# Fourteen interleaved units of each MLP without a loop; copies and sums of odd up groups moved ahead of the seventh product's splits

## What is computed

```python
def squared_relu_mlp(x, w1, w2):
    return jnp.square(jax.nn.relu(x @ w1)) @ w2
...
        h = layer_norm(DN_ALPHA * h + y, ln_g[i, 0], ln_b[i, 0])
        f = squared_relu_mlp(h, mlp_w1[i], mlp_w2[i])
        h = layer_norm(DN_ALPHA * h + f, ln_g[i, 1], ln_b[i, 1])
```

## Time and profile before

| what | us |
|---|---|
| median of 3 runs | 2150.74 |
| lowest and highest | 2150.31 and 2152.03 |
| profiled execution, its own time | 2150.6 |
| its span in the profile | 2148.9 |

### The profile page before, as it was taken

The page is one execution under the profiler, slowest core; times in us unless marked ns, Lnnn a source line. Parts: engine busy times, 40 slices in busy tenths (PEclk is TensorE's granted clock), DMA queues, the critical chain, the costliest instruction groups (busy, mean ns, idle before and its releaser), DMA issues.

```text
span 2148.9 us, 28041 instructions
## 1 busy us (share of the span) xinstructions
PE 2123.4 (99%) x10994; PEld 1817.2 (85%) x10994; DVE 1721.2 (80%) x1456; ACT 1163.7 (54%) x1034; POOL 185.5 (9%) x153
## 2 busy tenths in 40 slices
PE   9999999999999999999999999999999999999998
PEld 8888888988888888888888888889888888888886
DVE  5555559888988988989777666797988988989887
ACT  4444445456656655656554344445655656566562
POOL 3000000300000000000030111102000000000000
PEclk9999999999999999999999999999999999999999
DMA  9546547678988889888646544666789889888883
GB/s 304 176 140 204 171 151 242 198 233 239 258 245 267 241 229 285 233 246 223 247 158 217 180 156 157 236 213 215 209 242 269 255 230 259 251 246 250 228 267 137
DMA packets 237310, 478.51 MB, mean 223 GB/s; under 512 B 7616, under 2 KB 7616, under 8 KB 236176
## 3 DMA queue, kind: packets, MB, share of 16 engines
q1 hardware_dynamic: 204672, 406.09, 53.9%
q0 software_dynamic: 32096, 70.07, 17.8%
q10 hardware_dynamic: 432, 0.79, 0.1%
HBM read 474.81 MB, written 2.10 MB: 222 GB/s over the span
## 4 chain that ended last, share of the span: by engine, by line
PE 95%; DVE 2%; ACT 1%; issue 1%; DMA 0%; ACTq 0%; POOL 0%; DVEq 0%
PE ps L609 66%; PE ps L935 8%; PE ps L933 8%; PE ps L939 7%; PE ps L813 2%; PE ps L868 1%; PE ps L870 1%; PE ps L875 1%; ACT hi L1361 1%; DVE work L1982 1%; PE ps L680 1%; DVE lo L1950 0%; ACT work L1372 0%; DMA res<-in_x_dram 0%; DVE res L1740 0%
## 5 line engine op out<-in xcount | busy, mean ns | idle before, releaser
L609 PE MATMUL ps<-X,hi 128*128 128x512 f32 (+1 forms) x3008 | 699.8, 378 | 15.3 <-DVE work L1982 9.6
L609 PEld LDWEIGHTS ps<-X,hi 128*128 128x128 f32 x3008 | 549.0, 189 | 119.9 <-issue 14.4
L1361 ACT ACTIVATE hi<-raw 128x2048 fp32r<-128x2048 f32 x196 | 372.6, 1915 | 238.7 <-DVE raw L1964 146.3
L1950 DVE TENSOR_TENSOR lo<-raw,hi 128x2048 fp32r<-128x2048 f32 x196 | 443.6, 2286 | 14.5 <-PE ps L609 6.5
L1569 DVE TENSOR_TENSOR lo<-raw,hi 128x2048 fp32r<-128x2048 f32 x136 | 314.0, 2323 | 127.1 <-ACT hi L1159 125.6
L1159 ACT ACTIVATE hi<-raw 128x2048 fp32r<-128x2048 f32 x151 | 287.3, 1915 | 209.7 <-PE ps L609 163.2
L609 PE MATMUL ps<-X,lo 128*128 128x256 f32 x2816 | 387.1, 283 | 0.2 <-issue 0.2
L609 PEld LDWEIGHTS ps<-X,lo 128*128 128x128 f32 x2816 | 373.2, 191 | 13.1 <-issue 0.3
L1950 DVE TENSOR_TENSOR lo<-up_raw,hi 128x2048 fp32r<-128x2048 f32 x112 | 256.1, 2287 | 56.6 <-PE ps L609 32.6
L1345 ACT ACTIVATE hi<-up_raw 128x2048 fp32r<-128x2048 f32 x112 | 214.0, 1911 | 94.5 <-PE ps L939 83.7
L609 PE MATMUL ps<-hi,X 128*128 128x512 f32 x768 | 245.0, 394 | 0.0
(11 more groups left out here) (237 smaller groups left out, 2345.6 us busy)
## 6 DMA issues: line engine op xcount, KB each, us to landing
raw<-in_mlp_w_dram SPq DMA_DIRECT2D x144, 1024.0 KB, 7.6
up_raw<-in_mlp_w_dram SPq DMA_DIRECT2D x112, 1024.0 KB, 7.6
raw<-in_mlp_w_dram POOLq DMA_DIRECT2D x56, 1024.0 KB, 9.4
raw<-in_gla_w_in_dram SPq DMA_DIRECT2D x48, 1024.0 KB, 5.3
raw<-in_attn_w_qkv_dram SPq DMA_DIRECT2D x47, 1024.0 KB, 5.2
raw<-in_attn_w_o_dram SPq DMA_DIRECT2D x16, 1024.0 KB, 5.9
raw<-in_gla_w_o_dram SPq DMA_DIRECT2D x16, 1024.0 KB, 5.3
work<-in_ln_g_dram POOLq DMA_DIRECT2D x4, 1024.0 KB, 6.7
```

Source lines behind the costliest of these rows:

```text
L609: return pe.matmul(o, w, m, start=start, stop=stop)
L1361: act.activation(hi[:, P_AT[p] % 4], raw[:, slot], ACT.Copy).then_inc(hi_ready, 2 if p == PRODUCTS - 1 else 1)
L1950: dve.tensor_tensor(lo[:, at % 3], src, hi[:, at % 4].bitcast(F32), ALU.subtract).then_inc(lo_ready, n)
```

## The change

The loop over units 4 to 11 is gone on the three engines, and all fourteen units are written out. On ScalarE the copies of an odd unit (`right_halves(n, 1, 0, ...)`) stand ahead of `down_hi(m, i, c, 6)`. On VectorE the sums of an odd unit (`add_halves(n, 1, 0)`) and then `add_product(m, i, c, 4)` stand ahead of `down_lo(m, i, c, 6)`. Line numbers in the new kernel are lower by 5 to 11.

```diff
--- before.py
+++ after.py
@@ -1027,13 +1027,8 @@
                             w = mm(ps[:, 4 + i, 0:SEQ], lo[:, (j + 2) % 3, k, blk(i)], X[:, 4 * j + k, 0, :],
                                    False, 4 * j + k == KT - 1)
                     w.then_inc(w_used, 1)
-                for c in range(4):
-                    fused(m, c, c, c == 0)
-                with pe.Fori(1, FGS // 4) as it:
-                    for c in range(4):
-                        fused(m, 4 * it + c, c)
-                for c in range(FGS % 4):
-                    fused(m, FGS - FGS % 4 + c, c)
+                for i in range(FGS):
+                    fused(m, i, i % 4, i == 0)
                 g, r = g0 + 2 + FG * FGS, r0 + PRODUCTS * FGS
                 pe.wait_ge(res_added, r - 2)
                 rest_tiles(g, ((6, 7), (5, 4)), ((0, 0), (0, 1), (1, 0), (1, 1)),
@@ -1427,16 +1422,15 @@
                 up_hi(m, i, 3)
                 down_hi(m, i, c, 4)
                 down_hi(m, i, c, 5)
+                right_halves(n, 1, 0, used, k - 2, formed + 4)
                 down_hi(m, i, c, 6)
                 if end:
                     f = i + 1 + (G_MLP[m] + 2 - AHEAD_MLP[m])
                     split_hi(g + FG, 0, f)
-                    right_halves(n, 1, 0, used, k - 2, formed + 4)
                     split_hi(g + FG, 1, f)
                     squared_relu(n, 1, k, half)
                     return
                 up_hi(m, i + 1, 0)
-                right_halves(n, 1, 0, used, k - 2, formed + 4)
                 down_hi(m, i + 1, nxt, 0)
                 squared_relu(n, 1, k, half)
                 up_hi(m, i + 1, 1)
@@ -1453,13 +1447,8 @@
                 up_hi(m, 0, 1)
                 right_halves(n0 + 1, 1, 1, 4 * g0 + 8, None, None)
                 squared_relu(n0 + 1, 1, 32 * m + 2, 0)
-                for c in range(4):
-                    fused(m, c, c)
-                with act.Fori(1, FGS // 4) as it:
-                    for c in range(4):
-                        fused(m, 4 * it + c, c)
-                for c in range(FGS % 4):
-                    fused(m, FGS - FGS % 4 + c, c, True)
+                for i in range(FGS):
+                    fused(m, i, i % 4, i >= FGS - 2)
                 g, f = g0 + 2 + FG * FGS, f0 + 2 + FGS
                 split_hi(g, 2, f)
                 split_hi(g, 3, f)
@@ -2082,14 +2071,13 @@
                 add_product(m, i, c, 2)
                 down_lo(m, i, c, 4)
                 down_lo(m, i, c, 5)
+                add_halves(n, 1, 0)
+                add_product(m, i, c, 4)
                 down_lo(m, i, c, 6)
-                add_product(m, i, c, 4)
                 if last:
                     tail_lo(m, 0)
-                    add_halves(n, 1, 0)
                     return
                 up_lo(m, i + 1, 0)
-                add_halves(n, 1, 0)
                 down_lo(m, i + 1, nxt, 0)
 
             def tail_lo(m, j):
@@ -2116,17 +2104,9 @@
                 up_lo(m, 0, 0)
                 down_lo(m, 0, 0, 0)
                 add_halves(n0 + 1, 1, 1)
-                even_unit(m, 0, 0, True)
-                odd_unit(m, 1, 1)
-                even_unit(m, 2, 2)
-                odd_unit(m, 3, 3)
-                with dve.Fori(1, FGS // 4) as it:
-                    even_unit(m, 4 * it, 0)
-                    odd_unit(m, 4 * it + 1, 1)
-                    even_unit(m, 4 * it + 2, 2)
-                    odd_unit(m, 4 * it + 3, 3)
-                even_unit(m, FGS - 2, 0)
-                odd_unit(m, FGS - 1, 1, True)
+                for i in range(0, FGS, 2):
+                    even_unit(m, i, i % 4, i == 0)
+                    odd_unit(m, i + 1, (i + 1) % 4, i + 2 == FGS)
                 g, r = g0 + 2 + FG * FGS, RES_MLP[m] + PRODUCTS * FGS
                 add_product(m, FGS - 1, 1, 5)
                 add_product(m, FGS - 1, 1, 6)
```

## The result

The changed kernel takes 2129.99 us (median of 4 runs, 2129.61 to 2130.07), the kernel before beside it 2150.9; the ratio is 0.9902 [0.9885, 0.9919]. In a later session it was 2129.74 (2128.48 to 2130.07) against 2151.97.

The account below looks back on a forecast made before the run. TensorE, busy 2123.4 of 2148.9 us, bounds the kernel, so only its idle time can go: 12.7 us at ten borders plus 5.7 at two turns, 18.4. Profiled 2150.6 becomes 2132.2, median 2132.3 us, range 2130.3 to 2137.5.

Parts of the forecast that it names:

- Part 1, the loop: Turns of the loop, one per MLP: writing it out removes two taken TensorE branches, 5.05 - 1.92 = 3.1 us.
- The third "issue" wait: One of three TensorE "issue" waits totalling 5.3 us; the two others were the turns, this one a few tenths.
- its register work: Loop's register instructions computing waits' values on three engines: costed at nothing, as covered by work in the engines.
- Part 2, the order: Odd units: copies and sums ahead of the seventh product free ten borders, 9.6 + 10 x 0.31 = 12.7 us.
- Template times of the even unit: Even units' times behind product 4's start, put on unit 3: copies +0.20 to +1.29, half sums +0.84 to +2.13.
- Both in the units: Ten borders at 12.7 us and two turns, with both parts, at 5.7: sum 18.4 us.
- (a): Even units: the wait moves to product 1, whose slack was put at 0.4 us; 2137.0 to 2138.7; chance 0.13.
- (b): Turns: TensorE waits for instructions in straight code too, each turn keeps 1.7 us; 2135.7; chance 0.06.
- (c): Odd units: late copies make the seventh product late, 2.7 us in each of 14, 38 us; 2170; chance 0.03.
- (d): MLP transfers: if loads already set the pace, the time stays at 2150.7; chance 0.03.
- the clock is no part of the story: MLP windows showed a clock of 1.00, the upper level of 2.4 GHz, so no clock term was included.
- The 2 us of room below the forecast: Range's low side: for the third "issue" wait, shorter waits elsewhere and the spread of the runs.

Follow-up runs that it names:

- late_form: Changed kernel with the second form's sum (0.6 us) put ahead of the first form's low part in even units; 2136.48 us.
- loop_only: Changed kernel with the old order of copies and sums in odd units, so only the loop is written out; 2146.03 us.
- dve_only: Changed kernel with ScalarE's old order (late copies of the halves), VectorE's new order kept; 2170.48 us.
- before_look_a: The kernel before, unchanged, run again for a further profile; 2150.41 us.
- act_only: Changed kernel with VectorE's old order (late sums), ScalarE's early copies kept; 2149.48 us.
- loop_fill: loop_only plus 12 unread matmuls in TensorE's idle time ahead of the last six matmuls; 2143.16 us.

## Why the prediction was right and wrong

- **Part 1, the loop**: 3.1 us forecast, 3.8 measured with that part alone, from the same profile of before. The mechanism was right and the size a little low. The third "issue" wait, left out of the sum as "a few tenths", was a second stall of the turn (2.29 us of low half for 1.91), and the ordinary borders gained 0.3 without the loop, where the prediction had put its register work at nothing. With both parts, the turns were worth 6.0 us for a forecast of 5.7. The rule that a taken branch out of the fetched window stalls (the Trainium skill, "Runtime: NRT & Kernel Launch", section "Instruction fetch mechanics") agrees with the instruction packet within each of the 12 branches, which last 3.8 to 7.5 us. The figure of about 108 ns (the Trainium skill, "Advanced Engine Details and Errata", section "Control Flow Timing") does not.
- **Part 2, the order**: 12.7 forecast at ten borders, 12.6 in the profile of before, 12.5 measured alone. Template times of the even unit held within 0.1 us.
- **Both in the units**: 18.4 against 18.54. Shown by the fixed points, and by both parts alone and together. That they agree to 0.1 is in part luck: 0.3 too little at the turns and 0.1 too much at the borders, and the price of a turn differs by 0.8 us between runs.
- **Rivals**: (a) did not happen, and late_form shows how near it was, 0.36 us. (b) fell: loop_only has no "issue" wait at its borders. (c) is what dve_only does, at 39.9 us for 38. (d) fell: the loads did not hold the time at 2150.7.
- **The step that failed** is the sentence in the first part that "the clock is no part of the story". It rested on a window in the MLP, and the sum then put everything outside the units at nothing. The window at the end of the same trace had a clock of 0.66 and was not read. Outside the units the profiled run gained 1.91 us at the end, 1.70 by the clock and 0.21 by the last transfers, and 0.48 at the start, where the clock rose at 10.2 in place of 11.4 us. Without these 2.4 us the profiled time would have been 2132.0, within the range; with them the median fell 0.3 below its low end, 2130.3. The 2 us of room below the forecast were meant for waits and the spread of the runs, not for this. The two further profiles of before with a fall at a turn show that the loop was worth more than its branch in some runs.

Shown is that the clock differs and what it costs. Not shown is why it was high under the last six matmuls in both profiles of the changed kernel and low in three of four of the kernel before, with the same idle stretches. So this part of the gain is not shown to come from the change: before_look_a had the high clock there without it, and loop_only, act_only and dve_only, all without the loop, had the low one. Not shown either is that the unread matmuls keep it high, since 7 of the 13 profiles without them have it high too; for it speak all four profiles with them, and loop_fill, whose 5 runs all lie below the 7 of loop_only.

## What to carry to other kernels

Where the matrix engine is 99% busy, the gain of an edit can be read to a few tenths of a us from the step between two matmuls at a border with and without a stall; the slack of the next wait is worth the same care, since either engine's half of a reordering alone turned a gain of 15 us into a loss of 4 or of 25. Before a sum is closed, read the clock at both ends of the kernel and behind its longest stalls, not only in the stage that is changed. A taken branch over a long body is such a stall on the matrix engine's list: here, over four units, it cost 2.5 us and more, while the branches of this kernel's short loops lasted 0.25 us at most.

## What was not expected

- The clock can fall behind a stall of some 3 us at a loop's turn: window clocks of 0.50 to 0.77, the next tile's high half 5.29 us for 3.63. The kernel before spreads over 4.5 us in its 52 timed runs (2150.08 to 2154.61, median 2152.3), the changed one over 1.6 in 8 (2128.48 to 2130.07). The turns are a part of that and not all: act_only, without the loop, spreads over 4.0 in 10.
- With twelve matmuls that nobody reads in idle time at the end, the end of the kernel before took 6.4 us in place of 8.0; one of its four profiles without them took 6.4 too.
- The loop's branch took a different time at every turn (3.8 to 7.5 us, with waits of 1.8 to 3.6 us ahead of the tile), although the code is the same. Most of the difference is how late the instruction packet starts.
- The transfers that write the result land 0.2 to 0.3 us sooner in every profile of a kernel without the loop.
